# Order and waits of two weight buffers at the start of the experts' stage

## The reference, cut to what matters

```python
pg = softmax(x @ w_rg); grp = argmax(pg)               # one of 4 groups
le = (x @ w_re).reshape(T, 4, 8)[grp]                  # its 8 experts
top_l, top_i = top_k(le, 2)                            # two of them
top_w = softmax(top_l) * max(pg)
# for each expert e, on its tokens:
out = (silu(xb @ w_g[e]) * (xb @ w_u[e])) @ w_d[e]     # 1024->256, 1024->256, 256->1024
y = sum over the two experts of top_w * out
```

## Time and profile before

| | |
|---|---|
| three timed runs, median | 1551.4 us (1550.9 to 1553.43) |
| the profiled execution | 1556.95 us |
| its span | 1555.1 us |
| granted TensorE clock, mean | 0.964 |
| PE busy | 1425.6 us (92%) |
| PEld busy | 1092.0 us (70%) |
| DVE, ACT, POOL busy | 612.9, 335.2, 366.3 us |
| moved by DMA | 355.37 MB, mean 229 GB/s |

### The profile page before, as it was taken

One profiled execution on the slowest core, in us unless ns is written; L12 is line 12 of the kernel. 1 busy time (PEld: TensorE's weight loads), 2 busy tenths in 40 slices (PEclk: granted clock), 3 DMA queues, 4 the chain that ended last, 5 costly groups with the idle time before them and its releaser, 6 DMA issues.

```text
span 1555.1 us, 25254 instructions
## 1 busy us (share of the span) xinstructions
PE 1425.6 (92%) x9681; PEld 1092.0 (70%) x9681; DVE 612.9 (39%) x1453; ACT 335.2 (22%) x853; POOL 366.3 (24%) x471
## 2 busy tenths in 40 slices
PE   7999999898998999997899999999888989999964
PEld 5889899665887766563488889876577876556441
DVE  1121333578378322211452123348756852221116
ACT  2211211464111111110141121236430111111102
POOL 0100015542451312111010000754227321121101
PEclk9999999999998999998999999989899989999987
DMA  9410111674817999999642111157343499999974
GB/s 381 125 65 33 64 65 36 220 284 187 327 66 280 367 387 419 419 418 418 251 125 77 47 65 33 68 169 273 141 158 127 154 363 386 420 418 418 417 293 174
DMA packets 76741, 355.37 MB, mean 229 GB/s; under 512 B 20464, under 2 KB 23792, under 8 KB 43088
## 3 DMA queue, kind: packets, MB, share of 16 engines
q1 hardware_dynamic: 43056, 292.66, 47.8%
q0 software_dynamic: 20416, 46.73, 8.3%
q10 hardware_dynamic: 13152, 14.37, 2.9%
HBM read 341.25 MB, written 32.07 MB: 240 GB/s over the span
## 4 chain that ended last, share of the span: by engine, by line
PE 75%; DVE 8%; DMA 8%; issue 4%; POOL 3%; ACT 1%; SPq 1%; ACTq 0%; DVEq 0%; POOLq 0%
PE bank L1166 22%; PE bank L1531 15%; PE bank L1552 7%; DMA ring<-in_w_exp 4%; PE bank L1402 4%; PE bank L955 2%; PE bank L1150 2%; PE bank L858 2%; PE bank L1325 2%; DMA att<-mod_rows 2%; PE bank L1512 2%; PE bank L1299 1%; PE bank L1112 1%; PE bank L1115 1%; PE bank L881 1%
## 5 line engine op out<-in xcount | busy, mean ns | idle before, releaser
L1166 PE MATMUL bank<-ring,hT 128*128 128x256 f32 (+1 forms) x1600 | 340.9, 373 | 1.1 <-DVE z L2242 1.1
L1166 PEld LDWEIGHTS bank<-ring,hT 128*128 128x128 f32 x1600 | 293.5, 192 | 37.5 <-issue 1.6
L1531 PE MATMUL bank<-z,att 128*64 128x256 f32 (+2 forms) x960 | 181.0, 398 | 10.9 <-DMA ring<-in_w_exp 10.5
L1531 PEld LDWEIGHTS bank<-z,att 128*64 128x64 f32 (+2 forms) x960 | 118.8, 152 | 49.4 <-DMA ring<-in_w_exp 11.4
L1402 PE MATMUL bank<-ring,hT 128*128 128x256 f32 x640 | 142.7, 382 | 1.7 <-ACT hT L1838 1.1
L1402 PEld LDWEIGHTS bank<-ring,hT 128*128 128x128 f32 x640 | 121.2, 192 | 17.5 <-issue 2.0
L2693 DVE TENSOR_TENSOR att<-att,bank 128x256 f32<-128x256 f32 x36 | 15.2, 421 | 272.6 <-ACT att L1927 272.6
L3028 POOL DMA_INDIRECT expert_rows<-att,cur x36 | 37.1, 1030 | 357.4 <-DVE att L2706 348.2
L1531 PE MATMUL bank<-ring,att 128*64 128x256 f32 (+2 forms) x672 | 116.9, 413 | 3.7 <-issue 3.7
L1531 PEld LDWEIGHTS bank<-ring,att 128*64 128x64 f32 (+2 forms) x672 | 71.1, 146 | 21.4 <-issue 4.2
L2242 DVE COPY z<-bank 128x512 f32<-128x512 f32 (+3 forms) x35 | 20.1, 578 | 152.5 <-PE bank L1166 152.5
(11 more groups left out here) (407 smaller groups left out, 2372.8 us busy)
## 6 DMA issues: line engine op xcount, KB each, us to landing
z<-in_w_exp SPq DMA_DIRECT2D x74, 1024.0 KB, 22.2
ring<-in_w_exp SPq DMA_DIRECT2D x72, 1024.0 KB, 19.2
ring<-in_w_ada SPq DMA_DIRECT2D x41, 1024.0 KB, 6.1
ring<-in_w_in SPq DMA_DIRECT2D x24, 1024.0 KB, 5.0
hT<-in_w_exp SPq DMA_DIRECT2D x24, 1024.0 KB, 22.9
att<-in_w_exp SPq DMA_DIRECT2D x12, 1024.0 KB, 19.4
ring<-in_w_out SPq DMA_DIRECT2D x8, 1024.0 KB, 9.9
z<-expert_rows ACTq DMA_DIRECT2D x16, 512.0 KB, 8.6
```

The costliest lines, as they stand in the source:

```text
L1166: last = eng.matmul(bk[:, i * UN:i * UN + nw], hTv[:, k, t * P:(t + 1) * P], w[:, k, 0:nw], start=(k == 0), stop=(k == KD - 1))
L1531: last = eng.matmul(bank[2 + j][c * m_:(c + 1) * m_, u * DE:(u + 1) * DE], rows, wv[c][k // 4][:, k % 4, :], start=(k == 0), stop=(k == KD ...
```

## The change

The places of the split buffer (15) and of buffer 14 in the list are exchanged. Piece 15 now goes to the split buffer and waits for the second "hot" comparison. Piece 16 goes to buffer 14 and waits for "w12" and for a new event "asked". This event is raised on POOL by a memset of one column of a scratch tile, which stands between `gather(0)` and `gather(1)`. The wait for `gath0` at this place is gone. The two conditions on `i` become conditions on the buffer. The first line of the diff only gives the new event the semaphore of its group.

```diff
@@ STAGE
-        ("norm", (..., "diag", "hcol")),
+        ("norm", (..., "diag", "hcol", "asked")),
@@ -594,7 +594,7 @@
         POOL_OF = [pool_of_slots([s for s in range(RING) if s not in out_slots[l]] + [8, 9, 10] + out_slots[l]
-                                 + [12, 13, ONCE_SLOT, 6, 7, 11, 14, SPLIT_SLOT, LATE_SLOT])
+                                 + [12, 13, ONCE_SLOT, 6, 7, 11, SPLIT_SLOT, 14, LATE_SLOT])
                    for l in range(DEPTH)]
@@ -795,9 +795,11 @@
                     elif i == 14:
                         eng.wait_ge(*ev.at("full", jobs.number(("RL", l, NT - 1))))
-                    elif i == 15:
+                    elif n == SPLIT_SLOT and before[PIECES[i]] is None:
+                        eng.wait_ge(*ev.at("hot", l, 1))
+                    elif n == 14 and before[PIECES[i]] is None:
                         eng.wait_ge(*ev.at("w12", l))
-                        eng.wait_ge(W["gath0"], 16)
+                        eng.wait_ge(*ev.at("asked", l))
@@ -3048,6 +3050,7 @@
                 gather(0)
+                eng.memset(sm[:, 0, 0:1], 0.0).then_inc(*pool.event("asked", l))
                 gather(1)
```

More of the change, by code:

```diff
@@ L271 @@
         ("attn", ("esink", "negmax", "sinkarg", "pnorm", "biased", "rope_half", "rope", "vp", "bias")),
-        ("norm", ("lnhat", "lnvar", "lnnm", "lng", "lnrstd", "x1", "x2", "hsc", "h2", "comb", "lnneg", "lnsq", "lnsum", "lnmean", "oscaled", "u", "rows", "diag", "hcol")),
+        ("norm", ("lnhat", "lnvar", "lnnm", "lng", "lnrstd", "x1", "x2", "hsc", "h2", "comb", "lnneg", "lnsq", "lnsum", "lnmean", "oscaled", "u", "rows", "diag", "hcol", "asked")),
         ("route", ("r_ge", "r_ed", "r_gd", "r_dl", "assign", "hot", "ctl", "outrank", "place", "wx", "logits", "w12"))):
```

## The result

Over 22 runs each, the changed kernel has a median of 1557.76 us (1553.39 to 1561.64) and the kernel before 1553.32 us (1548.08 to 1558.16). The ratio is 1.0026 with a 95% interval of 1.0017 to 1.0036: 4.0 us slower, between 2.6 and 5.6. The median of before was 1551.4 us in the three runs that the prediction had; so the move is best read as the ratio.

The account below looks back on a forecast made before the run. PE's start of pass 0 and then the weight-load train were taken to bound the experts' stage. Direct gains 0, later gather landing +0.3 and +0.5 us, memset hidden: +0.8 us, 1552.3 us, range 1550.2 to 1556.5.

Parts of the forecast that it names:

- The bound: Experts' stage, each layer: PE's pass 0 start, then 33 us of PE, then the weight-load train set the end.
- the hole: DMA at 545 to 550 us, share 0.60: SP waits for pass 0's down product; early loads only lengthen it.
- The start of pass 0: PE at 515.02 us in layer 0: waits for DVE's copy, behind a 2.15 us cast ending with POOL's shifts.
- The slack of 6.9 and 6.7 us: Longest time from first gather's issue to landing that would not delay pass 0, layer 0 and layer 1.
- The early split loads and buffer 14: SP's queue: split 1 MB issued 8.6 us earlier, buffer 14's MB at about 507.9 us; direct gain 0 each.
- The memset: POOL, between the first two gathers: 0.1 us a layer, bounds 0 and 0.5; hidden if the gather lands later.
- g: First gather's time from issue to landing: taken as 7.2 us, costing 0.3 us in layer 0, 0.5 in layer 1.
- The argument of the short backlog: First gather would be issued behind little more than 1 MB, not 4 MB, which spoke against 8.1 us to landing.
- the 8.5 us from which I took two thirds: Upper value for the first gather's landing; 7.2 us was put two thirds of the way from 4.5 to it.
- The rule of the Trainium skill: DMA engines alternate queues by packet, so the first gather waits at most some 2.5 us extra: 7.0 us to landing.
- The rival of the clock: PE, idle from 512.12 us, falls to half clock in pass 0: 2.5 us a layer, 1557.2 us; chance 0.04.
- the crowded gather: First gather lands after 9.2 us, pass 0 2.3 and 2.5 us later: +4.8, 1556.2 us (11.5: 1560.8); chance 0.15.

Follow-up runs that it names:

- The run with later loads: Kernel before, with the two buffers and all loads behind them also waiting until PE has transposed the first gathered rows; ratio 1.0003.
- the two kernels with quiet gathers: Kernel before with only the memset added, its event waited for by nobody: 1.0015; kernel before with loads held until PE transposed the first rows: 1.0003.
- the kernel with more filler: Changed kernel with 24 instead of 16 filler calls (PE matmuls that keep it busy) before the first transposes; ratio 1.0037 against the kernel before.

## Why the prediction was wrong, point by point

*The bound* was right: the restart of the train hangs on PE's start of pass 0 and passes to the end. In the three profiles the restart moved by 2.8 to 5.3 us in layer 0 and the last load by 3.3 to 5.3. In the eleven profiles of the table whose restart lies at 40.8 us or later, the last load lands 189.5 to 190.8 us behind the restart, in both layers. The run with later loads shows that bytes ahead of the hole count for nothing. What the text did not say is how far this holds: the hole is 2 us deep (0.60 of 5 us), and with the start 2.2 to 2.4 us earlier and the late buffer's load 5 us later the last load came 191.9 and 192.1 us behind the restart: there the bytes had become the bound.

*The start of pass 0* was read right: POOL's shifts through DVE's cast, shown by 0.17 against 2.15 us. The slack of 6.9 and 6.7 us was 0.2 us too long: where the landing sets pass 0 and the transposes run at full clock, pass 0 begins 1.96 to 1.97 us behind it, which leaves 6.7 us in layer 0 (8.70 less 1.97) and 6.5 in layer 1 (8.47 less 1.97). In layer 1 a landing of 6.9 cost 0.44 us against the kernel before (0.5 forecast, for a landing of 7.2), or 0.2 us against the two kernels with quiet gathers that start pass 0 at 8.74; with the split buffer alone 7.0 cost 0.26 us in layer 0.

*The early split loads and buffer 14* were issued as forecast, 3.6 us ahead and 1.4 us behind the gather's issue. *The memset* took 0.12 us (0.1 forecast) and vanished in the gap.

*The term that failed is g*, the landing of the first gather in layer 0. I took 7.2 us, because the backlog would be short; it is 8.1, 9.1 and 8.6 us. In layer 1, where it is 6.9 to 7.2, the value was right. The argument of the short backlog counted the MB ahead only; that MB alone gives 7.0 us. Buffer 14's MB, which enters while the rows are moving, adds 1.1 to 2.1 us in layer 0 and 0 to 0.3 in layer 1. The nearest rows, 8.1 and 9.2 us of the third gather, were taken under just such a queue that is fed again while the gather runs, and should have been the value instead of the upper end. SP's timeline before shows it; the third gather is issued at 516.05:

```profile
510.95 0.33 SPq L760 DMA_DIRECT2D att<-in_w_exp  x1
512.05 0.34 SPq L758 DMA_DIRECT2D hT<-in_w_exp  x1
512.57 0.78 SPq L758 DMA_DIRECT2D att<-in_w_exp  x1
514.46 0.34 SPq L760 DMA_DIRECT2D z<-in_w_exp  x1
518.88 0.85 SPq L760 DMA_DIRECT2D ring<-in_w_exp  x2
```

These are 3 MB ahead of that gather, not the 4 MB by which I told it apart from the new case, and two more loads begin to go out 2.8 us behind it. Nor does the 8.5 us from which I took two thirds stand in any row.

The rule of the Trainium skill (DMA: Bandwidth & Descriptors, section "Queues, rings and completion order") gave 7.0 us by the wait for one load's share. For the MB ahead of the gather (7.0 and 6.9 us), and for layer 1 (6.9 to 7.2), the runs agree with it; in layer 0 the 8.1 to 9.1 us are above it.

*The rival of the clock* was held apart from the crowded gather, with 0.04. The runs show one case: a gather that lands late is what leaves PE idle. The sum had no term for the clock. In layer 0 the pass then took 8.6 to 9.6 us instead of 7.1, 1.4 to 2.4 us more, where the rival had 2.5 us in each layer; in layer 1 it took 7.1. So the right sum, by the means of the three profiles, was for layer 0 a landing of 8.6 us, by which pass 0 starts 2.0 us later, and 1.9 us for the clock, and for layer 1 a start 0.6 us later: 4.5 us instead of 0.8.

*The range* reached 5.1 us above the median that I had, and the move of 4.0 to 4.4 us is inside this; but that median, 1551.4 us of three runs, lay 1.9 us under the one of 22, and 1557.76 is above the 1556.5. The ratio applied to the median that I had would be 1555.4 us, near the 1556.2 of the crowded gather. A chance of 0.70 had been put on a case priced at 0.8 us, and 0.19 on all the slower ones, which was too little. The 1557.2 us of the rival of the clock lies close to the 1557.76 by luck: it rests on the low median and on a price that only one layer paid.

Open: why layer 0's landing is 1.2 to 2.0 us later than layer 1's in the changed kernel, with nearly the same MB of weights beside it (2.48 and 2.43). The steps of the landing narrow it: in the three profiles four to seven of the sixteen come after 6 us in layer 0, and one or two in layer 1. In layer 0 a packet of 16 KB on q8, of the kind that the DMA view calls instruction, takes 1.1 us at 3.1 to 3.6 us after the issue, in layer 1 none does; but with the split buffer alone it is there too, and the landing is 7.0 us, so it is not shown to be the cause. Also open: why the time of the kernel with more filler did not follow its stage.

## What to carry to other kernels

A load that can be issued earlier is worth something only if no later point of the load queue runs dry waiting for a consumer; look for a hole behind it first. Before a load is moved ahead of a small, urgent transfer, price that transfer by the rows where it already runs under load, not by the ones where it runs alone. If an engine then idles ahead of its restart, its clock belongs in the same sum.

## What the runs showed of the hardware

A gather of 128 rows of 4 KB took 4.2 to 4.7 us from issue to landing with little or nothing queued beside it, and 6.9 to 7.0 us with one MB of weight loads queued ahead of it. With a further MB issued 1.4 us behind it, it took 8.1 to 9.1 us in layer 0 and 6.7 to 7.2 us in layer 1. Its first row moved at 1.8 us in the first case and at 2.9 to 3.2 us in the others. The lateness is mostly that of the last few of the landing's sixteen steps: in all these loaded cases at least eight of them were done by 5.2 us.

A cast of 42 numbers on one partition took 2.13 to 2.16 us on DVE while POOL added 128x1024 tiles, and 0.17 us without, in every profile.

In four profiles in which PE had been idle for 2.0 to 4.0 us ahead of the eight transposes of layer 0, part of the next 64 matmuls ran at half clock (1.2 GHz, a granted 0.50) and they took 8.6 to 9.7 us. With 0.4 and 0.6 us idle in layer 0, and with 1.6 to 1.9 us in layer 1, they ran at full clock (2.4 GHz, 1.00) in 7.1 us.
